# Mixture-of-experts gather moved from one bulk stage into the expert loop, with 0/1 matrices in place of slot numbers

## The reference

```
scores = sigmoid(t @ w_router); biased = scores + router_bias      # t: 256 x 1024, 64 experts
# the 4 best of 8 groups of experts, then the 8 best experts of a token (TOP_K = 8)
w = scores[chosen]; combine = w / sum(w) * 2.5
gu  = t @ w_experts_gate_up[e]              # 1024 x 512 for each expert
act = silu(gu[:, :256]) * gu[:, 256:] * combine[:, e]
out = sum over e of act @ w_experts_down[e] # 256 x 1024 for each expert
out += (silu(t @ w_shared_gate_up)[:256] ...) @ w_shared_down      # one shared expert
```

## Time and profile before

| what | value |
|---|---|
| median of 3 runs | 718.59 us |
| the profiled execution's own time | 720.09 us |
| its span, first to last instruction | 718.3 us |
| TensorE matmul busy | 656.6 us, 91% of the span |
| VectorE busy | 306.0 us, 43% |
| ScalarE busy | 172.4 us, 24% |
| mean granted TensorE clock | 0.986 |
| read from memory | 224.31 MB |

### The profile page before, as it was taken

One profiled execution on the slowest core, in us unless ns is written; L12 is line 12 of the kernel. 1 busy time (PEld: TensorE's weight loads), 2 busy tenths in 40 slices (PEclk: granted clock), 3 DMA queues, 4 the chain that ended last, 5 costly groups with the idle time before them and its releaser, 6 DMA issues.

```text
span 718.3 us, 10083 instructions
## 1 busy us (share of the span) xinstructions
PE 656.6 (91%) x3371; PEld 368.0 (51%) x3371; DVE 306.0 (43%) x690; ACT 172.4 (24%) x309; POOL 33.2 (5%) x61
## 2 busy tenths in 40 slices
PE   2889999999999999999998988998989889898896
PEld 0568855888785486654443433443334333343333
DVE  2249948988266486432222222122222232222214
ACT  2020242213310241223212322133122221232211
POOL 7001100000000101000000000000000000000001
PEclk9999999999999999999999999999999999999999
DMA  8999987333404207338999999999999999999961
GB/s 302 387 387 378 387 299 282 116 119 118 147 20 171 103 3 321 148 133 313 426 429 427 426 428 420 429 425 425 432 420 431 423 426 432 423 427 425 423 276 58
DMA packets 43148, 225.65 MB, mean 314 GB/s; under 512 B 3504, under 2 KB 3536, under 8 KB 29430
## 3 DMA queue, kind: packets, MB, share of 16 engines
q1 hardware_dynamic: 41544, 224.43, 77.4%
q10 hardware_dynamic: 1582, 0.94, 0.4%
HBM read 224.31 MB, written 1.05 MB: 314 GB/s over the span
## 4 chain that ended last, share of the span: by engine, by line
PE 55%; DMA 34%; SPq 5%; DVE 4%; issue 1%; ACT 0%; POOL 0%; DVEq 0%; POOLq 0%
DMA raw<-n_w_experts_gate_up_dram 31%; PE bank L1539 14%; PE bank L1176 14%; PE bank L1487 4%; PE bank L1332 4%; PE bank L1372 4%; PE bank L1523 3%; DMA ring<-in_w_ada_dram 2%; PE bank L1222 2%; SPq L327 2%; PE bank L1529 1%; PE bank L1497 1%; SPq L334 1%; SPq L330 1%; PE bank L1547 1%
## 5 line engine op out<-in xcount | busy, mean ns | idle before, releaser
L1539 PE MATMUL bank<-raw,hT 128*32 128x512 f32 x832 | 99.4, 633 | 29.9 <-DMA raw<-n_w_experts_gate_up_dram 29.9
L1176 PE MATMUL bank<-work,ring 128*128 128x256 f32 x512 | 115.7, 381 | 1.8 <-ACT work L512 1.8
L1176 PEld LDWEIGHTS bank<-work,ring 128*128 128x128 f32 x512 | 95.7, 190 | 19.1 <-issue 6.4
L1523 PE MATMUL bank<-raw,hT 128*128 128x512 f32 x224 | 99.9, 599 | 0.3 <-DVE ST L1060 0.3
L1080 DVE TENSOR_TENSOR sg<-sg,bank 128x256 f32<-128x256 f32 x27 | 11.4, 421 | 177.7 <-ACT sg L664 177.7
L1539 PEld LDWEIGHTS bank<-raw,hT 128*32 128x32 f32 x832 | 30.6, 116 | 97.6 <-issue 97.6
L1523 PEld LDWEIGHTS bank<-raw,hT 128*128 128x128 f32 x224 | 41.4, 190 | 58.9 <-issue 58.1
L1497 PE MATMUL bank<-y,ST 128*128 128x512 f32 x224 | 70.5, 436 | 0.5 <-DVE y L1089 0.5
L664 ACT ACTIVATE sg<-bank 128x256 f32<-128x256 f32 x27 | 17.2, 635 | 210.8 <-PE bank L1539 120.6
L1065 DVE TENSOR_SCALAR SI<-iota,slotm,wt 128x32 f32 (+2 forms) x108 | 30.1, 315 | 56.4 <-issue 56.4
L1497 PEld LDWEIGHTS bank<-y,ST 128*128 128x128 f32 x224 | 39.0, 189 | 24.1 <-issue 17.6
(11 more groups left out here) (279 smaller groups left out, 575.3 us busy)
## 6 DMA issues: line engine op xcount, KB each, us to landing
raw<-n_w_experts_gate_up_dram SPq DMA_DIRECT2D x53, 2048.0 KB, 16.7
raw<-in_w_experts_down_dram SPq DMA_DIRECT2D x53, 1024.0 KB, 18.5
ring<-in_w_ada_dram SPq DMA_DIRECT2D x12, 2048.0 KB, 18.8
ring<-in_w_in_dram SPq DMA_DIRECT2D x8, 2048.0 KB, 14.3
ring<-in_w_out_dram SPq DMA_DIRECT2D x2, 2048.0 KB, 7.8
ring<-in_w_in_dram SPq DMA_DIRECT2D x2, 1024.0 KB, 18.9
ring<-in_w_attn_out_dram SPq DMA_DIRECT2D x1, 2048.0 KB, 9.0
ring<-in_w_conv_out_dram SPq DMA_DIRECT2D x1, 2048.0 KB, 7.6
```

The lines of the kernel that those rows point to most:

```text
L1176: ins = mm(b[:, at:at + SEQ], w[:, k, m * PART:(m + 1) * PART], h1T[:, k, :], start=(k == 0), stop=(k == KD - 1))
L1523: ins = mm(psU[:, :], hT[:, k, :], wg[:, k, :], start=(k == 0), stop=(k == KD - 1))
L1539: ins = mm(psU[c:c + 32, :], hT[:, k, c:c + 32], w_gu(s)[:, k, :], start=(k == 0), stop=(k == KD - 1))
```

## The change

The bulk gather, `hs`, `slotm`, `Emat`, `split` and the windows go. `place` holds each token's position within each candidate (from the rank matmul of line 1428, three DVE operations), and DVE makes the 0/1 matrix `SS` of a pass by comparing `place` with a row of numbers (`pick`). Before the loop, the 128 columns of the first big pass are gathered. In each pair, the big pass gathers 256 columns: those of the trio pass of the same pair and those of the next big pass. Four groups of eight fp32r matmuls of 256 columns go alternately to the two banks of `psY`, and ACT and DVE copy them to `hT`. The trio pass turns `SS` with TensorE for both passes (`turn_picks`): each time two transposes, and two fp32 matmuls of `SS` with the weights `wt`, 64 columns wide. DVE copies the transposes to `ST` and picks one column of the product as `wcol`. The copies of two passes stand apart (`ST[:, 0]`, `ST[:, 1]`). The second loop is gone: there are `n_trio` pairs and one last big pass. SyncE loads the first weights in another order and no longer waits for the gather. The diff, cut to its core:

```diff
-        y2 = sb("y2", [PART, 2, D], fp32r)
-        hT = sb("hT", [PART, KD, PART])
+        h2hi = sb("h2hi", [PART, TH, D], fp32r)
...
+        hT = view(work, 6144, KD * 2 * PART, KD)
+        SS = view(work_r, 9344, TH * 2 * PART, TH)
@@ block.sync
             load_gu(MID, es[0])
-            load_dn(MID, es[0])
+            sp.wait_ge(h2_ready, 4)
+            load_gu(SMALL[1], es[2])
             sp.wait_ge(*users[SHGU])
             load_gu(SMALL[0], es[1])
-            sp.wait_ge(gather_ps, 4 * KD)
-            load_gu(SMALL[1], es[2])
+            load_dn(MID, es[0])
+            sp.wait_ge(h2r_lo, 2)
+            load_dn(SMALL[1], es[2])
             sp.wait_ge(*users[SHD])
             load_dn(SMALL[0], es[1])
-            load_dn(SMALL[1], es[2])
...
-            with sp.Fori(n_trio, n_big) as g:
-                load_big(g)
+            load_big(n_trio)
@@ block.gpsimd
-            link(pool.tensor_scalar(nb, many[:, 0:1], 0.25, -0.625, ALU.mult, ALU.add))
+            link(pool.tensor_scalar(nb, many[:, 0:1], 0.25, 0.125, ALU.mult, ALU.add))
...
+            link(pool.tensor_scalar(na, many[:, 2:3], 0.5, -0.25, ALU.mult, ALU.add))
+            link(pool.tensor_scalar(na, na, WHOLE, -WHOLE, ALU.add, ALU.add))
+            link(pool.tensor_scalar(other, many[:, 1:2], -1.0, 2.0, ALU.add, ALU.max))
+            pool.tensor_scalar(tab[0:1, 0:1], nb, na, other, ALU.max, ALU.max).then_inc(tally_ready, 1)
@@ block.scalar
             with a.Fori(0, n_trio) as g:
                 a.wait_ge(big_gu, g + 1)
                 gate()
+                gathered(g + 1)
                 turned(g * 2)
-                trio_input(g)
-                outputs(g * 2, big_dn, g + 1)
+                gathered_late(g + 1)
+                outputs(1, g + 1, big_dn, g + 1)
@@ block.vector
+            def pick(j, c, n):
+                q = candidate_of(v, j)
+                for t in range(TH):
+                    ins = v.tensor_scalar(SS[:, t, c:c + n], iota[:, 0:n], place[:, t, bass.ds(q, 1)], None, ALU.is_equal)
+            def weights(j, w, c, n, b):
+                e = expert_of(v, j)
+                return v.tensor_copy(wcol[c:c + n, w:w + 1], b[c:c + n, bass.ds(e + SEQ, 1)])
+            def turned_big(g, sit, b):
+                v.wait_ge(sit_done, sit)
+                v.tensor_copy(ST[:, 1, :], b[:, 0:SEQ])
+                return weights(g, 1, 0, PART, b)
+            def turned_trio(g):
+                v.tensor_copy(ST[:, 0, :], psU[:, 0:SEQ])
+                for s, c, n in TRIO_WINDOWS:
+                    ins = weights(trio_rank(s, g, n_trio), 0, c, n, psU)
...
             with v.Fori(0, n_trio) as g:
                 product(g * 2)
-                trio_si(g)
-                outputs(g * 2)
+                gathered(g + 1)
+                gathered_late(g + 1)
+                outputs(g * 2, 1)
                 product(g * 2 + 1)
-                big_si(g + 1)
-                outputs(g * 2 + 1)
+                v.wait_ge(sit_done, g + 2)
+                turned_trio(g)
+                turned_big(g + 1, g + 2, psY[1]).then_inc(st_ready, 1)
+                pick_pair(g + 1)
+                outputs(g * 2 + 1, 0)
@@ block.tensor
+            def gather(b, ks, c, n):
+                for i, k in enumerate(ks):
+                    for s in range(2):
+                        for t in range(TH):
+                            ins = mm(b[:, i * n:(i + 1) * n], h2r[s][:, t, k * PART:(k + 1) * PART], SS[:, t, c:c + n],
+                                     start=(s == t == 0), stop=(s == 1 and t == TH - 1))
+                ins.then_inc(gather_ps, 1)
+            def turn_picks(c, b):
+                for t in range(TH):
+                    tr(b[:, t * PART:(t + 1) * PART], SS[:, t, c:c + PART].bitcast(fp32), ident[:, :])
+                for t in range(TH):
+                    ins = mm(b[:, SEQ:SEQ + E], SS[:, t, c:c + PART].bitcast(fp32), wt[:, t, :], start=(t == 0), stop=(t == TH - 1))
...
+            pe.wait_ge(pick_ready, 1)
+            pe.wait_ge(h2r_lo, 2)
+            gather(FIRST_B[0], range(0, 4), PART, PART)
+            gather(FIRST_B[1], range(4, KD), PART, PART)
+            turn_picks(PART, psM).then_inc(sit_done, 1)
...
             def big(i, g, first=False):
+                big_up(g)
+                pe.wait_ge(pick_ready, g + 2)
+                if first:
+                    shared_down([(t, n) for t in range(TH) for n in range(2)]).then_inc(shared_done, 1)
+                else:
+                    pe.wait_ge(y_lo, i * 2 + 1)
+                gather(psY[0], (0, 1), 0, 2 * PART)
+                gather(psY[1], (2, 3), 0, 2 * PART)
+                turn_act(i).then_inc(t_done, 1)
+                if not first:
+                    scatter(PASSES, 0)
+                pe.wait_ge(gather_act, g * 2 + 2)
+                gather(psY[0], (4, 5), 0, 2 * PART)
+                pe.wait_ge(gather_dve, g * 2 + 2)
+                gather(psY[1], (6, 7), 0, 2 * PART)
+                pe.wait_ge(gather_act, g * 2 + 3)
+                big_down(i, g, 0)
+                pe.wait_ge(gather_dve, g * 2 + 3)
+                big_down(i, g, 1)
             def trio(i, g):
...
+                pe.wait_ge(y_lo, i * 2 + 1)
+                scatter(PASSES, 1)
+                turn_act(i).then_inc(t_done, 1)
+                turn_picks(0, psU)
+                turn_picks(PART, psY[1]).then_inc(sit_done, 1)
+                pe.wait_ge(aT_ready, i + 1)
...
                 for n in range(2):
+                    if n == 1:
+                        pe.wait_ge(st_ready, g + 2)
                     for k in range(KF):
...
+            def last_big(i, g):
+                big_up(g)
+                pe.wait_ge(y_lo, i * 2 + 1)
+                turn_act(i).then_inc(t_done, 1)
+                scatter(PASSES, 0)
+                big_down(i, g, 0)
+                big_down(i, g, 1)
+            big(0, 0, first=True)
+            trio(1, 0)
+            with pe.Fori(1, n_trio) as g:
+                big(g * 2, g)
+                trio(g * 2 + 1, g)
+            last_big(n_trio * 2, n_trio)
```

More of the change, by code:

```diff
@@ L108, in hybrid_conformer_fox_moe_block @@
         st2 = sb("st2", [PART, 16])
-        wcol = sb("wcol", [PART, 1])
+        wcol = sb("wcol", [PART, 3])
         def view(t, at, n, k=None):
@@ L178, in hybrid_conformer_fox_moe_block @@
         perm = work[:, 5584:5712]
-        left, keycol, rank, startv = (work[:, 5712 + i:5713 + i] for i in range(4))
+        left, keycol, rank = (work[:, 5712 + i:5713 + i] for i in range(3))
         tcol = work[:, 5720:5723]
@@ L308, in hybrid_conformer_fox_moe_block @@
         MEAN_B = [6, 5]
+        FIRST_B = bank[4:6]
         ADA2_B = [7, 0, 7, 0, 7, 0, 7, 7]
@@ L369, in _ @@
                 load_big(g)
-                es = [expert_of(sp, trio_rank(s, g, n_big, n_trio)) for s in (MID,) + SMALL]
+                es = [expert_of(sp, trio_rank(s, g, n_trio)) for s in (MID,) + SMALL]
                 sp.wait_ge(trio_gu, g)
@@ L630, in _, with gathered, gathered_late @@
             a.wait_ge(tally_ready, 1)
[L631 to L661, removed]
+            n_trio = trio_count(a)
+            def gathered(n):
+                a.wait_ge(gather_ps, 4 * n - 1)
+                a.activation(hT[:, 0:2, :], psY[0][:, :].rearrange("p (k n) -> p k n", k=2), ACT.Copy).then_inc(gather_act, 1)
+            def gathered_late(n):
+                a.wait_ge(gather_ps, 4 * n + 1)
+                a.activation(hT[:, 4:6, :], psY[0][:, :].rearrange("p (k n) -> p k n", k=2), ACT.Copy).then_inc(gather_act, 1)
             def gate():
@@ L685, in _ @@
                 turned(g * 2 + 1)
[L686 to L693, removed]
+                outputs(0, g + 2, trio_dn, g + 1)
+            a.wait_ge(big_gu, n_trio + 1)
+            gate()
+            turned(n_trio * 2)
+            outputs(1, n_trio + 1, big_dn, n_trio + 1)
         @block.vector
@@ L1042, in _ @@
-            select(0)
+            v.tensor_scalar(perm, iota[:, 0:CAND], rank, None, ALU.is_equal).then_inc(tabs_ps_in, 1)
+            v.wait_ge(rank_done, 1)
+            link(v.scalar_tensor_tensor(place[:, :, 0:E], bank[3][:, 256:256 + TH * E].rearrange("p (t e) -> p t e", t=TH),
+                                        ABSENT, r["sel"], ALU.add, ALU.mult))
+            link(v.tensor_scalar(place[:, :, E:CAND], place[:, :, 0:E], -ABSENT - PART, None, ALU.add))
+            link(v.tensor_scalar(place[:, :, 0:E], place[:, :, 0:E], -ABSENT, None, ALU.add))
@@ L1043, in _ @@
+            pick(0, PART, PART).then_inc(pick_ready, 1)
+            h2_lo(1)
+            v.memset(wcol[:, 2:3], 0.0).then_inc(y_lo, 1)
             v.wait_ge(shg_ready, 1)
@@ L1429, in _ @@
             ins.then_inc(rank_done, 1)
-            pe.wait_ge(ecol_out, 1)
-            for c in range(0, CAND, E):
-                ins = mm(bank[3][c:c + E, 448:449], before[0:E, 0:E], ecnt[0:E, :], start=True, stop=True)
-            ins.then_inc(ecum_done, 1)
```

(26 more changed lines are left out.)

263 lines of the change are left out of this document (82 added, 181 removed).

## The result

The changed kernel takes 752.9 us (median of 4 runs, 750.46 to 753.86) against 718.59: ratio 1.046, 95% interval 1.044 to 1.0485. It is slower, as forecast, but by 34 us where the sum had 18.3. The profiled execution has 752.01 us and a span of 750.2.

The account below looks back on a forecast made before the run. The prediction took memory to bound the loop, with TensorE the bound after the change: -34.3 for the early start, +5.0, +6.4, +40.2 for twelve pairs and +0.9 gave about +18.3 us on 718.59, 736.9 us; range 718 to 753.

Parts of the forecast that it names:

- rival C: In the loop, the granted clock falls with each pair's wait, 1.8 of 32.7 us lost: 745 to 760 us; chance 0.11.
- the start: Ahead of the loop: the first up begins at 283.4 against 317.67, 34.3 us earlier.
- Bound and passes: In the loop: TensorE becomes the bound in place of memory; 14 big and 13 trio passes stay.
- The pair without the clock: One pair in the loop: 32.7 us, big pass 16.6 and trio pass 16.1, over 29.5 for its bytes.
- The gather in a pair: Big pass: 32 fp32r matmuls of 256 columns, 3.7 us plus 0.3 for handovers, 4.0 us added.
- The first pair: Start of the loop: no scatter in its big pass, whole shared down projection added, 37.7 us.
- the last pass: After the pairs: the last big pass takes 13.05 us and 0.9 more for silu and product no longer covered.
- The new wait: Before the trio's second down half: TensorE stands 2.1 us in every pair for VectorE's 3.9 us chain of picks.
- SyncE's loads: First weight loads in new order: no term in the sum, as nothing waits for weights in the first pair.
- The first gather: Before the loop: 32 fp32r matmuls of 128 columns at 0.22, 7.0 us (3.6 to 8).
- Rival A: Trio's second down half: the wait is covered, a pair takes 30.6 us and the whole 709.6 us; chance 0.12.
- Rival B: Gather in the loop: narrow matmuls don't get shorter, 3.6 us more in each pair, near 784 us; chance 0.07.

Follow-up runs that it names:

- e2_hoist: Changed kernel with VectorE loading all four expert numbers into registers before its waits for silu and the turned picks, order kept: 706.26 us, ratio 0.9815.
- e8_hoist_last: e2_hoist with six scatter matmuls put ahead of the act transposes in the last big pass: 705.09 us, ratio 0.979.
- e10_old_loads: e2_hoist with SyncE's first weight loads back in the old order, one behind the end of the first gather: 706.22 us.
- e4_high: Changed kernel with the low halves of the inputs left out of the gather, 16 instead of 32 matmuls in a pair: 736.97 us.
- e6_hoist1: Changed kernel with only one of VectorE's four register loads done ahead of the wait: 724.64 us.
- e3_fill: Changed kernel with 18 useless fp32r matmuls of 256 columns on TensorE in the wait before the trio's second down half: 738.39 us, ratio 1.027.

## Why the prediction came out as it did

The forecast of slower holds, and so does nearly the whole sum; the size does not. The range ended at 753, and the 752.9 us lie 0.1 us inside it, with two of the four runs above (753.79 and 753.86). That is luck: a term that the sum left out was worth 17 us, and it fits only because the range had taken in half of rival C and because the start came out 3.3 us earlier than forecast.

Right, by its own steps:
- *Bound and passes.* The loop passes from memory to TensorE, with the same 14 + 13 passes.
- *The pair without the clock*: 32.7 us forecast, 32.7 to 32.8 measured where no fall lies in it.
- *The gather in a pair.* 3.82 us for 32 matmuls (0.119 each), where the sum had 3.7 and 0.3 for handovers.
- *The first pair*, 37.8 against 37.7; the last pass, 13.95 us forecast and measured (e2_hoist), of which 1.1 is the uncovered silu and product (e8_hoist_last), against 0.9.
- *The new wait*, named with its place and its releaser and put at 2.1 us, measured at 2.07. Its cause, a register load of 0.8 us for each of four picks, is shown by taking one, two and all four out of it. The chain was 3.9 us as forecast, but otherwise made up: the picks took 0.9 us each, and the handovers from TensorE and back, put at 0.3 and 0.1, were 0.02 and 0.05.
- *SyncE's loads*, costed at nothing: e10_old_loads.

Wrong in size:
- *The clock.* The step that failed is the term for the wait, taken at its length alone. Rival C had the mechanism and the size (745 to 760 us) but a chance of only 0.11. Its price, measured, is 17 us in ten pairs; the start took 3.3 us back. What was held against rival C does not stand, as shown below.
- *The first gather.* 32 matmuls took 3.54 us, 0.111 each, the lower end of what was given; 0.22 was taken from the wide form. This made the start 3.3 us earlier than forecast and hid part of the clock's cost.

Against rival C the prediction said that "the wait is shorter" than the 3 us ones before. The pair of the earlier trace rows that it names speaks otherwise: 29.60 us with 27.61 busy leave 2.0 us idle, not 3, and the clock is 0.94. TensorE's timeline of the kernel before, at the trio's up, shows a long wait without a fall of the clock, a long one with a fall, and a short one with a fall:

```profile
386.15 7.07 PE L1539 MATMUL bank<-raw,hT 128*32 128x512 f32 x64 [3.02 <-DMA raw<-n_w_experts_gate_up_dram]
...
415.65 8.38 PE L1539 MATMUL bank<-raw,hT 128*32 128x512 f32 x64 [3.27 <-DMA raw<-n_w_experts_gate_up_dram]
...
445.17 8.77 PE L1539 MATMUL bank<-raw,hT 128*32 128x512 f32 x64 [1.97 <-DMA raw<-n_w_experts_gate_up_dram]
```

Of the 11 waits of 1.6 to 3.3 us in that trace five come with such a fall and six, three of 3.0 to 3.3 us among them, do not. There it cost nothing, as memory set the pair: 29.60 us with a clock of 0.94 and 29.60 with 1.00 (609.00 to 638.60 us). So the missing term could have been priced from the trace of before: up to 1.7 us (8.77 less 7.07) for a share of the pairs. What decides whether a wait of a given length is followed by a fall stays open.

Rival A, that the wait is covered, was not what the change did; e2_hoist made it so, and there the 709.6 us worked out for it became 706.3. By the spans (709.3 by the sum, 704.0 measured) 3.3 us of the difference are the first gather and 2.0 the pairs, 30.43 in place of 30.6. Rival B fell: narrow fp32r matmuls do get shorter, 0.119 us at 256 columns and 0.111 at 128, each with its own 128 columns of weights. The Trainium skill, page TensorE: Matmul & The Clock Gate, section The mechanism, has a sentence by which weight loads overlap a running matmul only in another row group; these rows disagree with it. The same section also lets a load into a background weight buffer go ahead, and that would fit them. Its section Back-to-back issue gap, by the formula for a single matmul, would have had 0.109 at 256 columns; the measured 0.119 is 9% more, and the halved row (0.116) was nearer.

What the early start is worth was not tried by itself; it is read from the two chains, 317.67 against 280.15.

## What to carry to other kernels

Work moved into a loop that waits for memory is free only up to the loop's slack: here 3.4 us a pair, against 4.3 us of gather and turning (the 30.43 of e2_hoist less 26.1) and, in the changed kernel, 2.3 for a wait and 1.7 for a fall of the clock. When a buffer is freed by a chain of small instructions, count the register loads between them; they cost more than the copies (3.87 us with four loads, 1.33 without), and an idle engine can do them ahead of its wait. Put ahead whatever another engine waits for first, and price a regular stall of TensorE by the clock behind it too: look in the trace at hand for what such a wait did to the granted clock, and fill the wait with useless matmuls as a quick test.

## What the hardware showed that was not expected

A wait of 2.07 us in each pair was followed by a granted clock of 1.2 GHz for 3.4 us in ten of 13 pairs of the changed kernel and in seven of 13 of e4_high; one of 1.2 us in none (e6_hoist1); in e3_fill, with the same hold-up but TensorE busy, in none either. Length alone does not decide it: in the kernel before a wait of 1.97 us had a fall behind it, and one of 3.02 us had none. The first fp32r matmuls of 128 columns came every 0.111 us, no slower than an fp32 instruction of that width (0.112). And with 512, 256 and 128 columns the fp32r forms take 0.232, 0.119 and 0.111 us: down to 256 the time follows the width, below that hardly.
